# Query projection with its gate columns last: the attention of the last head set moved into the gate units, in a two-block fp32 kernel on one core

## The chip, the cores and the metric

One core of a Trainium2 chip runs one launch. The metric is the device time of that launch in microseconds, the median of several runs. All matrix products are fp32 in three passes (see below), for one sequence of 256 tokens and a model width of 2048, so the kernel streams some 0.5 GB of weights from HBM once and the tensor engine works through them.

## What is computed

Two transformer-like blocks one after the other. The change touches the second half of the first block, a dilated window attention with a gate, and the work for the second block that is carried along beside it:

```python
# first block, attention layer (x is 256 x 2048; 16 heads of 128 in each of 3 dilation groups)
proj = rmsnorm(x, norm_b) @ w_in_b            # 2048 x 8192
q_all, gate = proj[..., :3*2048], proj[..., 3*2048:]
for g, (window, dilation) in enumerate(DILATED_PAIRS):
    q = apply_rope(q_all[:, :, g], cos, sin)
    o_g, lse_g = dilated_window_attention(q, k_shared, v_shared, window, dilation)
alpha = softmax(stack(lses), axis=0)
merged = sum(alpha * stack(outs))
x = x + (merged * silu(gate)) @ w_out_b
# for the second block: three products of silu(c) with ada_w (2048 x 3*2048, 2048 x 2*2048, 2048 x 3*2048)
shift, scale, gate = split(silu(c) @ ada_w + ada_b)
```

## The kernel before

**Units and blocks.** Every weight matrix is cut into blocks of 512 output columns, and a block into four units of 1 MB (four chunks of 128 rows by 512 columns, held as 128x2048). A unit is processed in two halves of two chunks. SyncE loads it into `raw[n % 2]`; ScalarE rounds a half to `w_hi` (`split_hi`, the instruction at L847); VectorE subtracts, `w_lo = raw - w_hi` (`split_lo`, L1426); TensorE then does 24 matmuls of 128x512 for the unit (`product`, L441), three for each chunk and each of the two token tiles. `w_hi` and `w_lo` have two slots as well: a half of unit n+2 can be written only when TensorE has finished that half of unit n (`half_used`). So in the step of unit q all engines work at units q (TensorE) and q+2 (ScalarE, VectorE).

**Banks.** A block sums into one of two pairs of PSUM banks, by the parity of its number. Before its first unit `product` waits (L417) until both tiles of the block two before it have been read out (`bank_free`).

**The query product `in_b`** has 16 blocks, in four sets of four: gate, group 0, group 1, group 2 of one set of four heads. The gate block is taken by ScalarE with a Silu into `gates` (which lies over the residual `res`, spilled to HBM before that and reloaded later), the other three are roped by VectorE (`rope`: four pieces a block, each three reads of PSUM and an add) into `rbuf`, turned by TensorE (`turn_q`) and copied by ScalarE to `q_t`. The four heads of a set are worked on during the 16 units of the next set, by the table `HEAD_STEPS`: in the step of each unit, after its matmuls, TensorE does `scores` (12 small matmuls, L578), `turn` (three transposes of the probabilities, L481) or `weigh` (L488 to L490). VectorE's part of the step comes first in its queue: for `weigh` it multiplies out (`take_out`, L1737), for `scores` it adds the mask (`mask_scores`, L1709); then it splits unit q+2, does one Ada step, and after that the maxima (L1715) or, one step after the scores, the sums over groups (`add_groups`, L1723 on).

**The last set's heads** run by `TAIL_STEPS` within the first six units of the output product `out_b`, whose unit order is changed for it, and from its step 6 on one after the other, with no matmuls of the product between them. `turn_heads` transposes the gated heads of a set, which become the input `xb` of `out_b`.

**Ada units.** 256 units of 512 KB hold the matrices of the second block's modulation. VectorE multiplies each with the silu row and sums (`add_ada`, L1437), one Ada unit beside one weight unit, from the first product to the end of `in_uz`; `ADA0` names the first Ada block of each stage. Four Ada columns are closed by `take_ada`. A load of an Ada unit is issued by SyncE behind the weight unit's and waits until the unit two before it has been used.

**Order.** Nothing is scheduled by a planner: every engine has one in-order queue, written out by hand with semaphores; sets 1 to 3 of `in_b` are one loop body.

Of the kernel before, what the change touches and what calls it, by code (L numbers as in the profile page):

```python
# [11 lines left out]
P = 128  # L12
# [55 lines left out]
def half_of(a, n, i):  # L68
# [13 lines left out]
TAIL_STEPS = {1: [("scores", 0)], 3: [("turn", 0), ("scores", 1)], 4: [("weigh", 0)],  # L82
              5: [("turn", 1), ("scores", 2)],
              6: [("weigh", 1), ("turn", 2), ("scores", 3), ("weigh", 2), ("turn", 3), ("weigh", 3)]}
# [11 lines left out]

HEAD_USES, TAIL_USES = uses_of(HEAD_STEPS), uses_of(TAIL_STEPS)

# [32 lines left out]
ADA0 = {"in_a": 0, "out_a": 4, "kv": 6, "in_b": 10, "out_b": 18, "in_v": 20, "in_uz": 24}  # L131
# [58 lines left out]
def build(nc, x, units, ada_units, vectors, tables, masks, pools, rope_2, spatial, norm_row, c_row, ln_rows, g_kr, g_qr, out):  # L190
    with ExitStack() as ctx:
# [52 lines left out]
        gates = res  # L244
# [30 lines left out]
        weighted, squared = sem("weighted"), sem("squared")  # L275
        factor_ready, scaled = sem("factor_ready"), sem("scaled")
# [32 lines left out]
        def _(sp):  # L309
# [43 lines left out]
            n0, m0 = UNIT0["grp"] + 4, UNIT0["grp"] + 2  # L353
# [4 lines left out]
            n0, pairs = n0 + 4, (ADA_UNITS - m0) // 2  # L358
            with Loop(sp, pairs) as j:
# [3 lines left out]
            n0 += 2 * pairs  # L363

            sp.dma_start(mask[:, 0:640], rope_2).then_inc(mask_in, 16)
            with Loop(sp, (UNITS - n0) // 2) as j:
                for i in range(2):
                    load_unit(n0 + i, 2, j)
            assert (UNITS - n0) % 2 == 0
# [29 lines left out]
        def _(pe):  # L399
# [166 lines left out]
            def turn_q(g, group, j):  # L566


                pe.wait_ge(roped, 5 + g + 3 * j + (3 if group >= 6 else 0))
                for i in range(2):  # L570
                    turn(g0 + group + i, tiles(rbuf, 2 * P * i), 8, j)

            def scores_1(h, k, j):

                for t, groups in ((0, (0, 1, 2)), (1, (0, 1)), (1, (2,))):
                    bank, n = use(k, 20, j), (t + 1) * P
# [6 lines left out]
            def head_part(part, h, uses, j):  # L583

                k = k0 + uses[part, h]
                if part == "scores":
                    if h == 0:
                        for g in (g0 + 4, g0 + 5):

                            pe.wait_ge(turn_free[g % 2], g // 2 + 2 + 4 * j)  # L590
                    scores_1(h, k, j)
                elif part == "turn":
                    turn_probs(use(k, 20, j), 1 + h + 4 * j, ubuf_flat)
                else:

                    weigh(use(k, 20, j), k0 + uses["turn", h], 10 * j, (4 * j + h) * P)

            def turn_heads(group, uses, j):

                k = k0 + uses["weigh", 3]  # L600
                pe.wait_ge(small_free[k % 2], k // 2 + 2 + 10 * j)
                for i in range(2):
                    turn(g0 + group + i, tiles(heads_out, 2 * P * i), 8, j)

            def set_step(q, j, heads):

                if heads:
                    if q == 1:
                        turn_q(2, 4, j)
                    for part, h in HEAD_STEPS.get(q, ()):  # L610
                        head_part(part, h, HEAD_USES, j)
                if q == 11:
                    turn_q(0, 6 if heads else 0, j)
                if q == 15:
                    turn_q(1, 8 if heads else 2, j)
                if q == 15 and heads:
                    turn_heads(10, HEAD_USES, j)
# [4 lines left out]

            for b in range(4):
                product("in_b", b, xa, then=lambda q: set_step(4 * b + q, 0, False), before=None if b else await_rows)
            with Loop(pe, 3) as j:
                for b in range(4):
                    product("in_b", 4 + b, xa, bs=4, us=16, j=j, then=lambda q: set_step(4 * b + q, j, True))

            def tail_step(q):

                if q == 0:
                    turn_q(2, 4, 3)
                for part, h in TAIL_STEPS.get(q, ()):
                    head_part(part, h, TAIL_USES, 3)


            for b in range(2):
                product("out_b", b, xb, qs=range(3), n0=3 * b, then=lambda q: tail_step(3 * b + q))
            tail_step(6)
            turn_heads(6, TAIL_USES, 3)  # L640
            for g in (TURN0["xg"] - 2, TURN0["xg"] - 1):
                pe.wait_ge(turn_free[g % 2], g // 2 + 2)
            for b in range(2):
                product("out_b", b, xb, qs=(3,), n0=6 + b)
# [7 lines left out]
            product("out_b", 2, xb, then=turn_sum)  # L652
            product("out_b", 3, xb, then=lambda q: turn_sum(4 + q) if q < 2 else None)
# [182 lines left out]
        def _(act):  # L836
            steps = Chain(act, act_steps)

            def split_hi(n0, us=0, j=0):
# [3 lines left out]
                act.wait_ge(raw_in[n0 % 2], 16 * (n0 // 2 + 1) + 8 * us * j)  # L843
                for i in range(2):
                    if n0 >= 2:
                        act.wait_ge(half_used, 2 * (n0 - 2) + i + 1 + 2 * us * j)
                    act.activation(half_of(w_hi, n0, i), half_of(raw, n0, i), ACT.Copy).then_inc(hi_done, 1)  # L847
# [198 lines left out]
            def copy_q(g, group, j):  # L1046
                for i in range(2):
                    at = NT * NB + (4 * g + 2 * i) * S
                    copy_turned(g0 + group + i, side_flat[:, at:at + 2 * S], gs=8, j=j)

            def split_heads(group, j):
                for i in range(2):
                    hi_of(g0 + group + i, lambda cc: chunk(xb, 4 * j + 2 * i + cc), gs=8, j=j)

            def set_step(q, j, heads):

                if heads:
                    for part, h in HEAD_STEPS.get(q, ()):
                        if part == "turn":
                            copy_probs(k0 + HEAD_USES[part, h], 20, j)  # L1060
                split_hi(UNIT0["in_b"] + q + 2 + (16 if heads else 0), 16, j)
                if q == 4:

                    b0 = BLOCK0["in_b"] + (4 if heads else 0)
                    act.wait_ge(half_used, 2 * (UNIT0["in_b"] + 4 + (16 if heads else 0)) + 32 * j)
                    for t in range(NT):
                        at = (j + 1 if heads else 0) * NB
                        dst = gates[:, t, at:at + NB] if isinstance(at, int) else gates[:, t, bass.ds(at, NB)]
                        act.activation(dst, banks[2 * (b0 % 2) + t][:], ACT.Silu, scale=stat[:, 4 + t:5 + t])\
                            .then_inc(bank_free[b0 % 2], 1)  # L1070
                if heads:
                    if q == 1:
                        copy_q(2, 4, j)
                    for part, h in HEAD_STEPS.get(q - 1, ()):
                        if part == "scores":
                            exponents(1 + h + 4 * j, ubuf_flat, 768)
                if q == 11:
                    copy_q(0, 6 if heads else 0, j)
                if q == 15:
                    copy_q(1, 8 if heads else 2, j)  # L1080
                if q == 15 and heads:
                    split_heads(10, j)

            act.wait_ge(spilled, 16)
            for q in range(16):
                set_step(q, 0, False)
                if q == 2:

                    act.wait_ge(root_row, 1)
                    act.activation(rows[:], rows[:], ACT.Sqrt, bias=eps).then_inc(root_row, 1)  # L1090
            with Loop(act, 3, steps) as j:
                for q in range(16):
                    set_step(q, j, True)
            for q in range(6):
                if q < 5:
                    split_hi(UNIT0["out_b"] + q + 2)
                if q == 0:
                    copy_q(2, 4, 3)
                for part, h in TAIL_STEPS.get(q, ()):
                    if part == "turn":  # L1100
                        copy_probs(k0 + TAIL_USES[part, h], 20, 3)
# [1183 lines left out]
```

## Time and profile before

| | |
|---|---|
| median of 3 runs | 2192.15 us (2191.84 to 2194.24) |
| the profiled execution | 2189.68 us, its span 2188.0 us, granted TensorE clock 0.986 |
| TensorE busy | 2110.7 us, 96% of the span, 9732 matmuls and transposes |
| VectorE, ScalarE busy | 1574.4 us (72%), 1097.3 us (50%) |
| chain of work that ended last | TensorE 86%, VectorE 5%, ScalarE 4%, issue 2%, DMA 2% |
| HBM read | 518.01 MB, 239 GB/s over the span |

The span is nearly all TensorE. Its idle time is what an edit of the order can win, and it has to be looked up by stretch of time: the page gives 40 slices, and two slices near the middle (the 18th and the 20th) show less than nine tenths of TensorE. The trace shows which instruction stood there and who released it. In the trace a matmul's end is modelled and overlaps the next; the distance from start to start is its cost, about 0.227 us for 128x512 at full clock.

### The profile page before, as it was taken

How to read it: one execution, taken by the hardware profiler on the slowest of the kernel's cores; microseconds unless marked ns; L12 is line 12 of the kernel's file. 1: busy time of each engine (PE TensorE's matmuls, PEld its weight loads, DVE VectorE, ACT ScalarE, POOL GpSimd, SP SyncE). 2: the span in 40 equal slices, each digit the busy share in tenths (PEclk: the TensorE clock that was granted, in tenths of full speed). 3: DMA queues.
4: the chain of work that ended last, by engine and by line, in shares of the span. 5: the costliest groups of instructions: out<-in, count | busy, mean ns of one | idle time of the engine just before them, and what ended most of it. 6: DMA issues, size and time to landing. Idle time of an engine off the chain costs nothing.

```text
span 2188.0 us, 29739 instructions
## 1 busy us (share of the span) xinstructions
PE 2110.7 (96%) x9732; PEld 1746.1 (80%) x9732; DVE 1574.4 (72%) x2506; ACT 1097.3 (50%) x1683; POOL 11.6 (1%) x25
## 2 busy tenths in 40 slices
PE   7999999999999999979899999999999979999988
PEld 6888888888887878757788888888888868878867
DVE  5766777787879888857787778778765565556654
ACT  5444554445444444436544445454444365867742
POOL 0000000000000000000000000000000000000000
PEclk9999999999999999979999999999999989999999
DMA  7876678878766666647688777778744536433333
GB/s 294 293 281 252 239 276 320 301 283 289 264 254 235 228 256 227 222 166 259 232 296 297 289 296 298 278 293 285 301 185 173 192 125 240 173 131 139 136 134 134
DMA packets 93395, 523.34 MB, mean 239 GB/s; under 512 B 10337, under 2 KB 10593, under 8 KB 47489
## 3 DMA queue, kind: packets, MB, share of 16 engines
q1 hardware_dynamic: 90736, 509.60, 63.8%
q0 software_dynamic: 2032, 8.46, 1.1%
q10 hardware_dynamic: 544, 4.19, 0.5%
q8 instruction: 51, 0.84, 0.1%
q14 instruction: 32, 0.25, 0.0%
HBM read 518.01 MB, written 4.19 MB: 239 GB/s over the span
## 4 chain that ended last, share of the span: by engine, by line
PE 86%; DVE 5%; ACT 4%; issue 2%; DMA 2%; DVEq 0%; SPq 0%; ACTq 0%
PE bank L441 78%; PE bank L459 2%; DMA raw<-units 2%; DVE w_lo L1426 1%; PE bank L578 1%; ACT w_hi L847 1%; DVE ada_raw L1437 1%; PE bank L682 1%; PE bank L481 0%; PE bank L784 0%; PE bank L782 0%; PE bank L475 0%; PE bank L515 0%; DVE rbuf L1542 0%; PE bank L488 0%
## 5 line engine op out<-in xcount | busy, mean ns | idle before, releaser
L847 ACT ACTIVATE w_hi<-raw 128x1024 fp32r<-128x1024 f32 (+2 forms) x702 | 726.0, 1047 | 899.2 <-PE bank L441 665.8
L1426 DVE TENSOR_TENSOR w_lo<-raw,w_hi 128x1024 fp32r<-128x1024 f32 (+2 forms) x702 | 832.9, 1207 | 409.5 <-ACT w_hi L847 407.1
L441 PE MATMUL bank<-w_hi,xa_hi 128*128 128x512 f32 x1952 | 770.9, 395 | 5.6 <-DVE w_lo L1426 2.8
L441 PE MATMUL bank<-w_hi,xa_lo 128*128 128x512 f32 x1952 | 761.6, 390 | 0.0
L441 PE MATMUL bank<-w_lo,xa_hi 128*128 128x512 f32 x1952 | 761.2, 390 | 0.0
L441 PEld LDWEIGHTS bank<-w_hi,xa_hi 128*128 128x128 f32 x1952 | 367.7, 188 | 82.8 <-issue 6.1
L441 PEld LDWEIGHTS bank<-w_hi,xa_lo 128*128 128x128 f32 x1952 | 367.2, 188 | 77.6
L441 PEld LDWEIGHTS bank<-w_lo,xa_hi 128*128 128x128 f32 x1952 | 367.7, 188 | 74.6
L441 PE MATMUL bank<-w_hi,xb_hi 128*128 128x512 f32 (+2 forms) x864 | 336.9, 390 | 6.6 <-DVE rbuf L1563 3.6
L441 PE MATMUL bank<-w_hi,xb_lo 128*128 128x512 f32 (+2 forms) x864 | 330.2, 382 | 0.0
L441 PE MATMUL bank<-w_lo,xb_hi 128*128 128x512 f32 (+2 forms) x864 | 330.0, 382 | 0.0
L441 PEld LDWEIGHTS bank<-w_hi,xb_hi 128*128 128x128 f32 x864 | 165.0, 191 | 37.5 <-DVE rbuf L1563 4.0
L441 PEld LDWEIGHTS bank<-w_hi,xb_lo 128*128 128x128 f32 x864 | 164.4, 190 | 29.8
L441 PEld LDWEIGHTS bank<-w_lo,xb_hi 128*128 128x128 f32 x864 | 164.9, 191 | 28.8 <-issue 0.7
L1437 DVE CUSTOM_DVE_ANT_0 ada_raw<-ada_raw,silu_row,ada_acc 128x1024 f32<-128x1024 f32 x128 | 163.6, 1278 | 0.1
L1437 DVE CUSTOM_DVE_ANT_0 ada_raw<-ada_raw,silu_row 128x1024 f32<-128x1024 f32 x128 | 155.9, 1218 | 2.1 <-ACT silu_row L956 2.1
L927 ACT ACTIVATE small<-bank 128x384 f32<-128x384 f32 x32 | 15.7, 491 | 103.8 <-PE bank L481 103.8
L459 PE MATMUL bank<-tab,rbuf 128*128 128x128 f32 (+1 forms) x248 | 34.4, 279 | 9.4 <-DVE rbuf L2045 5.4
L578 PE MATMUL bank<-wide,side 128*128 (+2 forms) x192 | 38.9, 347 | 3.5 <-DVE small L1709 3.0
L459 PEld LDWEIGHTS bank<-tab,rbuf 128*128 128x128 f32 (+1 forms) x248 | 28.8, 139 | 15.7 <-DVE rbuf L2045 5.5
L578 PEld LDWEIGHTS bank<-wide,side 128*128 128x128 f32 x192 | 29.7, 199 | 8.5 <-DVE small L1709 5.0
L2121 DVE TENSOR_TENSOR small<-bank,mask 128x384 f32<-128x384 f32 x16 | 8.9, 557 | 37.0 <-PE bank L784 23.5
(237 smaller groups left out, 1241.3 us busy)
## 6 DMA issues: line engine op xcount, KB each, us to landing
raw<-units SPq DMA_DIRECT2D x351, 1024.0 KB, 4.8
ada_raw<-ada_units SPq DMA_DIRECT2D x256, 512.0 KB, 5.5
rows<-ln_rows POOLq DMA_DIRECT2D x8, 512.0 KB, 3.8
res<-x SPq DMA_DIRECT2D x4, 512.0 KB, 7.6
held<-res ACTq DMA_DIRECT2D x1, 2048.0 KB, 11.9
rows<-norm_row POOLq DMA_DIRECT2D x2, 1024.0 KB, 6.2
res<-held ACTq DMA_DIRECT2D x1, 2048.0 KB, 7.8
out<-res SPq DMA_DIRECT2D x4, 512.0 KB, 7.5
```

The costliest lines, as they stand in the source:

```text
L441: last = pe.matmul(ps[t][:, 0:cols], l, r, start=c == 0 and k == 0, stop=c == CPU * units_of - 1 and k == 2)
L459: last = pe.transpose(bank[0:n, at:at + P], src, ident)
L578: last = pe.matmul(bank[:, i * n:(i + 1) * n], q_t[:, 4 * g + h, t * P:(t + 1) * P], at_(keys_flat, (4 * j + h) * S, n), start=True, stop= ...
L682: last = pe.matmul(bank[:, i * S:(i + 1) * S], ws[:, i * P:(i + 1) * P], vmix[:, t, bass.ds(NB * j + i * S, S)], start=True, stop=True)
L847: act.activation(half_of(w_hi, n0, i), half_of(raw, n0, i), ACT.Copy).then_inc(hi_done, 1)
L927: act.activation(probs_t, small_bank[k0 % 2][:, 0:384], ACT.Copy).then_inc(small_free[k0 % 2], 1)
L1426: dve.tensor_tensor(half_of(w_lo, n0, i), half_of(raw, n0, i), half_of(w_hi, n0, i), ALU.subtract)\
L1437: dve.tensor_tensor_reduce(out=ada_raw[m0 % 2][:], in0=ada_raw[m0 % 2][:], in1=silu_row[:, m0 % 2 * 2 * NB:(m0 % 2 + 1) * 2 * NB], scale=1 ...
L2121: dve.tensor_tensor(small[:, 0:384], small_bank[k % 2][:, 0:384], mask[:, 0:384], ALU.add)\
```

## The change

- `in_b` now computes 12 query blocks first (four sets of three, 12 units each) and the four gate blocks last (16 units). The heads of set j-1 run in the 12 units of set j; those of the last set run in the gate units. `HEAD_STEPS` is a new, tighter table, and `TAIL_STEPS` and the changed unit order of `out_b` are gone.
- `take_out` writes un-gated heads into rows (`weighed`, over `res`) with one scalar factor. After each gate block ScalarE puts Silu into `rbuf` (`take_gate`) and VectorE multiplies (`apply_gate`) into `heads_out`; TensorE turns that (`turn_heads`). For the last gate block all this falls into the first unit of `out_b`. The reload of `res` is issued by ScalarE's queue in the second.
- VectorE's rope of group 0 is spread over the steps of units 4 to 7, one piece each, that of group 1 over units 9 and 10, that of group 2 over the first step of the next set.
- Ada units go by the table `ADA_STEPS`: eight in a set of 12 units, none beside the gate units; the 32 that are left over go to the eight blocks of `out_g`, which had none.
- `in_b` is written out on all engines, with no loop.

```diff
-HEAD_STEPS = {2: [("scores", 0)], 5: [("turn", 0), ("scores", 1)], 6: [("weigh", 0)],
-              8: [("turn", 1), ("scores", 2)], 9: [("weigh", 1)], 11: [("turn", 2), ("scores", 3)],
-              12: [("weigh", 2)], 13: [("turn", 3)], 14: [("weigh", 3)]}
-TAIL_STEPS = ...
+HEAD_STEPS = {2: [("scores", 0)], 4: [("turn", 0), ("scores", 1)], 5: [("weigh", 0)],
+              6: [("turn", 1), ("scores", 2)], 7: [("weigh", 1)], 8: [("turn", 2), ("scores", 3)],
+              9: [("weigh", 2)], 10: [("turn", 3)], 11: [("weigh", 3)]}
+SET_UNITS, GATE_UNITS = 12, 16
-ADA0 = {"in_a": 0, "out_a": 4, "kv": 6, "in_b": 10, "out_b": 18, "in_v": 20, "in_uz": 24}
+ADA0 = {"in_a": 0, "out_a": 4, "kv": 6, "in_b": 10, "out_b": 14, "in_v": 16, "in_uz": 20, "out_g": 28}
+ADA_STEPS = [{0: 1, 1: 1, 2: 1, 3: 1, 5: 1, 7: 1, 8: 1, 11: 1}] + 3 * [{1: 2, 2: 1, 3: 1, 8: 1, 10: 1, 11: 2}] + [{}]
...
# TensorE
+            def set_step(j, q):
+                if j and q == 1:
+                    turn_q(2, j - 1)
+                for part, h in HEAD_STEPS.get(q, ()) if j else ():
+                    head_part(part, h, j - 1)
+                if j < 4 and q in (8, 11):
+                    turn_q((q - 8) // 3, j)
+                if j == 4 and q in (5, 9, 13):
+                    turn_heads((q - 5) // 4)
...
+            for j in range(4):
+                for b in range(3):
+                    product("in_b", 3 * j + b, xa, then=lambda q: set_step(j, 4 * b + q),
+                            before=None if j or b else await_rows)
             for b in range(4):
+                product("in_b", 12 + b, xa, then=lambda q: set_step(4, 4 * b + q))
+            product("out_b", 0, xb, before=await_heads, then=lambda q: turn_heads(3) if q == 0 else None)
...
# ScalarE
+            def take_gate(b):
+                act.wait_ge(half_used, 2 * (UNIT0["in_b"] + 4 * SET_UNITS + 4 * b + 4))
+                if b:
+                    act.wait_ge(gated, b)
+                par = (GATE_BLOCK0 + b) % 2
+                for t in range(NT):
+                    act.activation(rbuf[:, t, :], banks[2 * par + t][:], ACT.Silu, scale=stat[:, 4 + t:5 + t]) ...
...
+                if q == 0:
+                    take_gate(3)
+                elif q == 1:
+                    split_heads(3)
+                    act.wait_ge(gated, 4)
+                    act.dma_start(res[:], held).then_inc(reloaded, 16)
...
# VectorE
+                for part, h in now:
+                    k = k0 + 20 * (j - 1) + HEAD_USES[part, h]
                     if part == "weigh":
+                        take_out(h, k, j - 1)
                     elif part == "scores":
+                        mask_scores(k)
+                if j and q == 0:
+                    rope_query(j - 1, 2, ((0, 0), (0, S)))
+                lo_half(n, 0)
+                for part, h in now:
                     if part == "scores":
+                        maxima(k0 + 20 * (j - 1) + HEAD_USES[part, h])
+                for part, h in before:
+                    if part == "scores":
+                        add_groups(h, j - 1)
+                lo_half(n, 1)
+                if j and q == 0:
+                    rope_query(j - 1, 2, ((1, 0), (1, S)))
+                if j < 4 and 4 <= q < 8:
+                    rope_query(j, 0, ((q // 2 - 2, q % 2 * S),))
+                if j < 4 and q in (9, 10):
+                    rope_query(j, 1, ((q - 9, 0), (q - 9, S)))
+                if j == 4 and q in (4, 8, 12):
+                    apply_gate(q // 4 - 1)
+                if j == 4 and q in (5, 9, 13):
+                    split_heads((q - 5) // 4)
+                for i in range(ADA_STEPS[j].get(q, 0)):
+                    add_ada(m + i)
...
-                after("out_g", n)
+                after("out_g", n, ada=8 * ADA0["out_g"] + 4 * n, then={3: lambda: take_ada(ADA0["out_g"] + n // 2)} if n % 2 else None)
```

## Rows read from the trace of the kernel before

**Rows 1.** Windows: us, busy time of each engine (instructions), granted clock, DMA share, GB/s

```profile
499.65:588.51 88.86, 88.86 (x403) 73.73 (x402) 70.82 (x103) 42.89 (x47) 0.00 (x0) 1.00 0.78 283
588.51:694.62 106.11, 104.36 (x503) 86.42 (x502) 91.00 (x168) 50.98 (x68) 0.00 (x0) 1.00 0.66 242
...
906.73:948.93 42.20, 39.69 (x189) 32.35 (x188) 34.38 (x70) 16.31 (x25) 0.00 (x0) 1.00 0.60 218
948.93:976.65 27.72, 13.44 (x59) 10.53 (x59) 15.61 (x36) 7.94 (x17) 0.00 (x0) 0.66 0.34 126
976.65:1036.62 59.97, 59.97 (x264) 49.11 (x264) 39.39 (x49) 34.37 (x62) 0.00 (x0) 0.96 0.66 242
```

**Rows 2.** Chain in order of time: start, us, engine and line, instructions

```profile
411.03 43.54 PE bank L441 x192
...
712.12 2.02 PE bank L578 x12
...
730.51 0.33 PE bank L481 x3
730.84 2.14 PE bank L578 x12
...
738.47 0.22 PE bank L488 x2
...
811.95 0.87 PE bank L459 x8
```

**Rows 3.** Waits of TensorE, 590 to 977 us: releaser, total us, times, longest

```profile
PE bank L578 <- DVE small L1709: 3.0, 3, 1.0
PE bank L459 <- ACT side L881: 2.3, 3, 0.8
```

**Rows 4.** Timeline of VectorE in set 2: start, us, line, op, idle before

```profile
739.30 0.61 DVE L1737 SCALAR_TENSOR_TENSOR side<-bank,stat,res 128x128 f32<-128x128 f32 x2 [0.69 <-PE bank L490]
739.82 2.35 DVE L1426 TENSOR_TENSOR w_lo<-raw,w_hi 128x1024 fp32r<-128x1024 f32 x2
742.09 1.22 DVE L1437 CUSTOM_DVE_ANT_0 ada_raw<-ada_raw,silu_row 128x1024 f32<-128x1024 f32 x1
...
743.24 0.28 DVE L1723 TENSOR_TENSOR small<-small 128x128 f32<-128x128 f32 x1
...
744.51 1.20 DVE L1426 TENSOR_TENSOR w_lo<-raw,w_hi 128x1024 fp32r<-128x1024 f32 x1
...
758.05 0.42 DVE L1529 TENSOR_TENSOR rbuf<-bank,tab 128x256 f32<-128x256 f32 x1
...
758.59 0.28 DVE L1533 TENSOR_TENSOR ubuf<-bank,tab 128x128 f32<-128x128 f32 x1
...
759.36 0.42 DVE L1529 TENSOR_TENSOR rbuf<-bank,tab 128x256 f32<-128x256 f32 x1
```

**Rows 5.** A split on ScalarE's timeline; a 128x512 product among VectorE's groups

```profile
738.51 1.06 ACT L847 ACTIVATE w_hi<-raw 128x1024 fp32r<-128x1024 f32 x1 [1.66 <-PE bank L441]
...
L1989 DVE TENSOR_TENSOR ubuf<-ubuf,rbuf 128x512 f32<-128x512 f32 x16 | 10.3, 687 | 0.1
```

**Rows 6.** Timeline of TensorE around three idle times

```profile
914.36 1.23 PE L459 MATMUL bank<-tab,rbuf 128*128 128x128 f32 x8 [1.91 <-DVE xb_lo L1486]
...
1927.96 1.97 PE L459 MATMUL bank<-tab,rbuf 128*128 128x128 f32 x8 [4.29 <-DVE rbuf L2045]
...
2133.32 0.79 PE L441 MATMUL bank<-w_hi,xb_hi 128*128 128x512 f32 x1 [3.60 <-DVE rbuf L1563]
...
2138.61 0.53 PE L441 MATMUL bank<-w_hi,xb_hi 128*128 128x512 f32 x1
```

**Rows 7.** Timeline of ScalarE while the residual is spilled to HBM

```profile
345.57 2.01 ACT L847 ACTIVATE w_hi<-raw 128x1024 fp32r<-128x1024 f32 x2 [6.81 <-DMA raw<-units]
```

**Rows 8.** Timelines of VectorE and ScalarE at the end of `out_g`

```profile
1772.16 1.29 DVE L1568 TENSOR_TENSOR res<-res,rbuf 128x512 f32<-128x512 f32 x2
...
1774.96 0.61 ACT L908 ACTIVATE side<-res 128x512 f32<-128x512 f32 x1
```

More of the change, by code:

```diff
@@ L357, in _ @@
             sp.dma_start(mask[:], masks).then_inc(mask_in, 16)
-            n0, pairs = n0 + 4, (ADA_UNITS - m0) // 2
-            with Loop(sp, pairs) as j:
+            with Loop(sp, (UNIT0["in_b"] - UNIT0["out_a"]) // 2) as j:
+                for i in range(2):
+                    load_unit(UNIT0["out_a"] + 4 + i, 2, j)
+                    load_ada(m0 + i, 2, j)
+            n0, m0 = UNIT0["in_b"] + 4, 8 * ADA0["in_b"] + 2
+            for table in ADA_STEPS:
+                for q in range(SET_UNITS if table else GATE_UNITS):
+                    load_unit(n0)
+                    n0 += 1
+                    for _ in range(table.get(q, 0)):
+                        load_ada(m0)
+                        m0 += 1
+            with Loop(sp, (UNIT0["out_g"] - UNIT0["out_b"]) // 2) as j:
                 for i in range(2):
@@ L362, in _ @@
                     load_ada(m0 + i, 2, j)
-            n0 += 2 * pairs
+            n0, m0 = UNIT0["out_g"] + 4, 8 * ADA0["out_g"] + 2
             sp.dma_start(mask[:, 0:640], rope_2).then_inc(mask_in, 16)
+            with Loop(sp, (ADA_UNITS - m0) // 2) as j:
+                for i in range(2):
+                    load_unit(n0 + i, 2, j)
+                    load_ada(m0 + i, 2, j)
+            n0 += ADA_UNITS - m0
             with Loop(sp, (UNITS - n0) // 2) as j:
@@ L591, in head_part @@
                     scores_1(h, k, j)
                 elif part == "turn":
-                    turn_probs(use(k, 20, j), 1 + h + 4 * j, ubuf_flat)
+                    turn_probs(use(k), 1 + h + 4 * j, ubuf_flat)
                 else:
[L596 to L601, printed above, removed]
+                    weigh(use(k), k0 + 20 * j + HEAD_USES["turn", h], 0, (4 * j + h) * P)
@@ L602, in turn_heads @@
+            def turn_heads(b):
+                pe.wait_ge(gated, b + 1)
                 for i in range(2):
[L603 to L617, printed above, removed]
+                    turn(g0 + 24 + 2 * b + i, tiles(heads_out, 2 * P * i))
@@ L623, in _ @@
             for b in range(4):
[L624 to L634, printed above, removed]
@@ L637, in _, with await_heads @@
[L637 to L644, printed above, removed]
+                product("in_b", 12 + b, xa, then=lambda q: set_step(4, 4 * b + q))
+            def await_heads(q):
+                for i in range(2):
+                    g = g0 + 24 + 2 * q + i
+                    pe.wait_ge(turn_free[g % 2], g // 2 + 2)
@@ L650, in turn_sum @@
                 turn(TURN0["xg"] + g, tiles(res, 2 * P * g))
-            product("out_b", 2, xb, then=turn_sum)
-            product("out_b", 3, xb, then=lambda q: turn_sum(4 + q) if q < 2 else None)
+            for b in range(1, 4):
+                product("out_b", b, xb, then=lambda q: turn_sum(2 * b - 2 + q) if q < 2 else None)
             for g in (6, 7):
@@ L1044, in _, with copy_q @@
             k0, g0 = SMALL0["in_b"], TURN0["q"]
-            def copy_q(g, group, j):
+            def copy_q(g, j):
                 for i in range(2):
                     at = NT * NB + (4 * g + 2 * i) * S
-                    copy_turned(g0 + group + i, side_flat[:, at:at + 2 * S], gs=8, j=j)
-            def split_heads(group, j):
-                for i in range(2):
[L1053 to L1099, printed above, removed]
+                    copy_turned(g0 + 6 * j + 2 * g + i, side_flat[:, at:at + 2 * S])
@@ L1740, in take_out, with rope_query @@
                 last.then_inc(small_free[k % 2], 1)
-            def before_split(q, table, uses, j):
-                for part, h in table.get(q, ()):
-                    k = k0 + uses[part, h]
+            def rope_query(j, g, pieces):
+                n = 3 * j + g
+                b0 = BLOCK0["in_b"] + n
+                dve.wait_ge(half_used, 2 * (UNIT0["in_b"] + 4 * n + 4))
+                dve.wait_ge(turned, g0 + 2 * n)
+                rope([banks[2 * (b0 % 2) + t] for t in range(NT)], b0, 0, 0, pieces)
@@ new lines, in apply_gate, with split_heads @@
+            def apply_gate(b):
+                dve.wait_ge(bank_free[(GATE_BLOCK0 + b) % 2], read_out(GATE_BLOCK0 + b))
+                if b == 3:
+                    dve.wait_ge(small_free[(k0 + 79) % 2], small_read(k0 + 79))
+                for t in range(NT):
+                    last = dve.tensor_tensor(heads_out[:, t, :], weighed[:, t, b * NB:(b + 1) * NB], rbuf[:, t, :], ALU.mult)
+                last.then_inc(gated, 1)
+            def split_heads(b):
+                for i in range(2):
+                    lo_of(g0 + 24 + 2 * b + i, xb, 4 * b + 2 * i, HI0["o"] + 2 * b + i + 1)
@@ L1746, in before_split, with set_step @@
+            def set_step(j, q, m):
+                n = UNIT0["in_b"] + SET_UNITS * j + q + 2
+                now, before = (HEAD_STEPS.get(i, ()) if j else () for i in (q, q - 1))
+                for part, h in now:
+                    k = k0 + 20 * (j - 1) + HEAD_USES[part, h]
                     if part == "weigh":
-                        take_out(h, k, j)
+                        take_out(h, k, j - 1)
                     elif part == "scores":
-                        mask_scores(h, k, j)
@@ L1751, in after_split @@
-            def after_split(q, table, uses, j):
-                for part, h in table.get(q, ()):
-                    if part == "scores" and not (table is TAIL_STEPS and q == 5):
-                        maxima(h, k0 + uses[part, h], j)
-                for part, h in table.get(q - 1, ()):
-                    if part == "scores":
-                        add_groups(h, j)
-            def split_heads(group, j):
-                for i in range(2):
-                    lo_of(g0 + group + i, xb, 4 * j + 2 * i, HI0["o"] + i + 1, gs=8, hs=2, j=j)
@@ new lines, in set_step @@
+                if j < 4 and q in (9, 10):
+                    rope_query(j, 1, ((q - 9, 0), (q - 9, S)))
+                if j == 4 and q in (4, 8, 12):
+                    apply_gate(q // 4 - 1)
+                if j == 4 and q in (5, 9, 13):
+                    split_heads((q - 5) // 4)
+                for i in range(ADA_STEPS[j].get(q, 0)):
+                    add_ada(m + i)
+            m0 = 8 * ADA0["in_b"]
+            for j in range(5):
+                for q in range(SET_UNITS if j < 4 else GATE_UNITS):
+                    if j == 1 and q == 0:
+                        dve.wait_ge(spilled, 16)
+                    set_step(j, q, m0)
+                    m0 += ADA_STEPS[j].get(q, 0)
+                    if j == 0 and q == 1:
+                        dve.wait_ge(row_in, 16)
+                        dve.tensor_tensor(rows[:], rows[:], rows[:], ALU.mult).then_inc(root_row, 1)
+                if j < 4:
+                    take_ada(ADA0["in_b"] + j)
@@ L2246 @@
         blocks(a["w_k"], a["w_v"]),
-        blocks(*[w_in_b[:, i * D:(i + 1) * D] for i in (3, 0, 1, 2)]),
-        out_b[out_order],
+        blocks(*[w_in_b[:, i * D:(i + 1) * D] for i in range(3)]),
+        units(w_in_b[:, 3 * D:], NB, CPU),
+        out_b,
         blocks(a_w_in[:, 2 * D:4 * D]),
```

226 lines of the change are left out of this document (98 added, 128 removed).

## The prediction, made before the changed kernel was run

> **What bounds the kernel now.** The page first: TensorE is busy for 96% of the span, so an edit of the order can win or lose only the time in which TensorE stands. I cut the span into stretches, one for each set of `in_b` and for the parts of `out_b` [rows 1]. The first set (16 units, no heads) is all TensorE: 88.86 us. The three sets with heads take 106.1 us each (the second and third repeat the row, up to 906.73). Then come the 42.2 us in which `out_b` runs its first units beside the heads of the last set, 27.7 us with TensorE at work for only 13.4 and a granted clock of 0.66, and 60 us of plain `out_b`. The chain gives the prices of TensorE's work [rows 2]: 192 matmuls in 43.54 us, so 5.44 for a unit of 24; scores 2.02, a turn with scores behind it 0.33 + 2.14 = 2.47, a weigh 3 x 0.22 = 0.67, a turned pair 0.87. The four heads of a set are 2.02 + 3 x 2.47 + 0.33 + 4 x 0.67 = 12.4. A check on the first set: 16 x 5.44 + 2 x 0.87 = 88.8, as the row has it.
>
> **What the change removes.** A set of before holds 87.1 + 12.4 + 4 x 0.87 = 103.0 us of work and takes 106.1; 3.1 are lost. The waits name 3.0 + 2.3 = 5.3 us for the three sets together [rows 3]: the third bank of the fourth head's scores waits for VectorE, and the gated heads' turn waits for a bank that ScalarE is copying. Both go, since the scores are spread otherwise and the heads' turn no longer follows another turn: 5.3. The other 1.3 or so of a set (slower steps at the change of instruction kinds) goes with the heads and stays. From 906.73 to 1036.62 it is 129.9 us for 16 units, the heads, a pair of q, the pair of gated heads and six half pairs of sums: 87.1 + 12.4 + 0.9 + 0.9 + 2.6 = 103.9. Of the 26.0 lost, 1.3 stay; 24.7 go. All TensorE work is the same in number after the change. **Removed: 30.0 us.**
>
> **The new wait at unit 8 of each set.** A set now has three blocks. Block 2 (units 8 to 11) needs the banks of block 0 (units 0 to 3), and these are read out by four pieces of rope in VectorE's steps 4 to 7. The last piece stands in step 7 behind the second half of the split of unit 9, and this half can't be rounded before TensorE has finished unit 7. So TensorE reaches unit 8 before the piece has begun, whatever VectorE's load. In set 0, from the end of unit 7: ScalarE begins 0.04 later (738.47 to 738.51) and takes 1.06 [rows 2, 5], the subtraction 1.20, the three reads of a rope piece 758.05 to 758.87 = 0.82 [rows 4], a semaphore about 0.1: 3.2 us. In sets 1 to 3 step 7 begins with `take_out(1)`, which waits for the weigh behind unit 7. In the trace the same step stands at 738.47: the weigh follows the unit, `take_out` starts at 739.30, the next split at 739.82, 1.35 after the unit's end [rows 4]. Then half of unit 9, 1.14 (2.27 for the two), `add_groups(2)`, 1.27 (743.24 to 744.51), the second half, 1.14, and the reads, 0.82: 5.7 after the unit's end, with the semaphore 5.8, against the 0.5 at which the next matmul would be issued behind the weigh. 5.3 us, three times. The sum is 3.2 + 15.9 = **19.1 us**, all on TensorE's path. Queued behind that wait are all later matmuls, and so everything.
>
> **The boundary between sets.** VectorE had 91.0 us of work in 106.1 [rows 1]; it now has, for 12 units, 12 x 2.27 + 8 x 1.15 for Ada + 12 pieces of rope at 1.3 + some 20 for heads = 72 in a set with 80 of TensorE's work, but unevenly. From the end of unit 9 in a set with heads (us after it): split begins 1.35, half 2.5, sums 3.8, half 4.9, two pieces of rope 7.5. Step 10: the split of unit 12 waits until ScalarE, which first copies the probabilities of the turn behind unit 10, has rounded it, 8.0; both halves 10.3, two pieces 12.9, Ada 14.1. TensorE ends unit 11 at 0.67 + 5.44 + 0.33 + 5.44 = 11.9, its weigh at 12.5, and waits 0.4 for rope. Step 11 and step 0 of the next set in VectorE's queue: `take_out` 14.6, two halves 16.9, two Ada units 19.2, `take_ada` 19.6, two pieces 22.2, two halves 24.5, two pieces 27.1. TensorE turns at 13.8, does two units until 24.7 and wants the third turned pair: 2.4 us wait. Sets 1 to 3 pay the 0.4 at their end, sets 2, 3 and the gate units the 2.4, and set 1, behind a set with no heads and one Ada unit in step 11, about 0.8: 1.2 + 7.2 + 0.8 = **9.2 us**. The least is near nothing, if the queues overlap a little better (the nearest row is `out_b`'s first unit, where the same turn waits 1.91 for VectorE after four pieces of rope [rows 6]); the most is 14, if the second Ada unit of step 11, whose load is issued only when step 10's is used, comes late by 1.6.
>
> **The first unit of `out_b`.** `turn_heads(3)` stands behind unit 0, and needs `apply_gate(3)`, which stands in VectorE's step 0 behind the second half of a split that again waits for the end of the unit. ScalarE 1.1, half 1.2, Ada 1.15, two products 128x512 at 0.69 [rows 4, 5]: **4.9 us**. ScalarE's Silu lies beside the unit's matmuls and costs nothing; if that cover were gone it would be some 1.3. The same steps in the gate units have a whole unit between product and turn and are hidden, at 0.
>
> **The clock.** After 1.91 us idle a turn of eight takes 1.23, little over the usual [rows 2, 6]. After 4.29 us it takes 1.97: that stretch is at the lower level, 1.2 GHz instead of 2.4. After 3.60 us thirteen matmuls, until 2138.61, run at the lower level, at 0.43 instead of 0.23: 2.6 lost. The three waits of 5.3 and the one of 4.9 are longer than either. I take 2.0 each, between the about 1.4 and the 2.6: **8.0 us**, bounds 3 and 12.
>
> **What is moved elsewhere.** Ada: 32 steps leave `in_b`'s shorter sets and its gate units and land in `out_g`, where VectorE works 57% of the time; 1.15 more in each 5.44 is hidden by the matmuls, and the load beside a weight unit is what `in_b` had in its first set, 283 GB/s with no wait [rows 1]. Only the last Ada step and `take_ada` of `out_g` come before the last residual add, some 1.5 us; that add ended at 1773.4 while ScalarE, busy with its own part, took up its result at 1774.96 [rows 8]: +0.2, bounds 0 and 1.6. SyncE's queue: an Ada load waits for its buffer in front of the next unit's load, but in sets 1 to 3 only where VectorE is late itself. The 2 MB reload of the residual used to run while TensorE stood; now it meets two streams. Its nearest row is the spill, during which ScalarE waited 6.81 us for a weight unit [rows 7], with almost all of it taken up by the unit ahead: +1.0, bounds 0 and 4. The Trainium skill (Trainium Kernel Development and Optimization, Key Constraints) says that the DMAs of all queues run on the same 16 engines and interleave, which speaks against issuing this reload beside the loads; the row agrees. Without that rule this term would be 0. Writing `in_b` out instead of looping and Exp no longer alternating with Silu on ScalarE's tables are free: neither stands on the path.
>
> **Sum:** -30.0 + 19.1 + 9.2 + 4.9 + 8.0 + 0.2 + 1.0 = +12.4 us. The profiled execution took 2189.68, so 2202.1; the median of the three runs is 2.5 higher, 2192.15, and the forecast is 2192.15 + 12.4 = 2204.6 us.
>
> **Rivals.** (1) *The clock holds through waits of 5 us.* Then 8.0 go: 2196.6, at the edge of slower. Against it stand both rows of 3.60 and 4.29. 12%. (2) *The boundary is worse*: the second Ada unit is late, the waits before the third turned pair pass 4 us and cost clock too, and the reload costs its most: +5 + 4 + 3: 2216. For it: two Ada units in one step, with one of the loads issued 4 us before. 15%. (3) *VectorE's queue is shorter than I add up*, so that at unit 8 only the forced 3.2 us remain in every set and the boundary is 1: -30.0 + 12.8 + 1 + 4.9, 2.0 of clock for `out_b` alone, and 1.2, make -8.1: 2184, faster. It decides once `take_out` to the last read takes under some 3 us in all; against it, my durations are already from start to start. 8%. (4) *It doesn't do what it says*: the last set's attention is not covered by the gate units, since its probabilities wait for a Silu and a table change on ScalarE; then part of the 24.7 comes back, over 2210; 3%. (5) A mild mix, clock at its least and boundary near nothing, is 2192, no change: 8%. The forecast itself has 54%.
>
> **The numbers.** The range must reach from the mild mix to rival 2: 2190 to 2218. A difference under 0.2% (4.4 us) can't be told from none here. Faster: rival 3 and a little of the mix, 0.09. Within 0.2%: the rest of the mix and half of rival 1, 0.14. Slower: 0.77.
>
> **What would show it.** Right: in each set one idle time of TensorE before a matmul, released by VectorE's L1529 to L1533 kind (rope), 3.2 us in set 0 and 5.3 in the next three, with some ten matmuls at 0.63 long behind each; a turn behind unit 1 waiting 2 us for rope; 4.9 us before the turn in `out_b`; nothing of the old 27.7 us stretch. Wrong: no idle time at unit 8; matmuls at 0.39 long right behind it; or `out_g` longer than before.

## The result

The changed kernel takes 2205.14 us, median of 5 runs (2204.34 to 2207.32), against 2192.15 (2191.42 to 2197.85): a ratio of 1.006, 95% interval 1.0048 to 1.0072. It is 13.0 us slower. The forecast was 2204.6.

The profile after, first the stretches: most of set 0 (its first 65.6 us), two of the sets with heads, the gate units with the last set's heads, and `out_b` to its end. Columns: us; busy time of TensorE, weight loads, VectorE, ScalarE and GpSimd with their instructions; granted clock, DMA share, GB/s.

```profile
500.42:566.00 65.58, 62.45 (x281) 51.48 (x280) 47.13 (x68) 30.17 (x34) 0.00 (x0) 1.00 0.73 258
...
657.50:749.50 92.00, 84.04 (x398) 69.70 (x397) 70.82 (x141) 35.24 (x50) 0.00 (x0) 0.96 0.51 183
749.50:841.50 92.00, 84.42 (x398) 69.94 (x397) 70.93 (x142) 36.23 (x51) 0.00 (x0) 0.96 0.51 183
841.50:950.00 108.50, 105.98 (x517) 88.58 (x517) 76.17 (x133) 56.57 (x79) 0.00 (x0) 1.00 0.49 175
950.00:1057.48 107.48, 95.66 (x428) 78.24 (x426) 72.98 (x96) 56.77 (x96) 0.53 (x1) 0.95 0.73 267
```

The 27.7 us in which TensorE worked for 13.4 [rows 1] are gone: the gate units hold the last set's heads and TensorE is busy for 98% of them. But each set of 12 units, 80 us of work, takes 92, with a clock of 0.96 where before it was 1.00. Who is waited for, on TensorE from 499 to 1060 us (releaser: us in total, times, longest):

```profile
PE bank L462 <- DVE ubuf L1534: 18.3, 4, 5.1
PE bank L480 <- DVE rbuf L1543: 7.9, 6, 2.6
PE bank L480 <- DVE side L1755: 4.8, 1, 4.8
```

None of the three is in [rows 3]. The first line is a matmul (L462 is `product`) that waits for the last PSUM read of a rope piece, once in each of the four sets; the second, turned pairs that wait for rope; the third, the turn in `out_b` that waits for `apply_gate`. How the first looks, in set 0 and in set 2, on TensorE's timeline (start, us, line; idle before):

```profile
547.34 0.50 PE L462 MATMUL bank<-w_hi,xa_hi 128*128 128x512 f32 x1 [3.13 <-DVE ubuf L1534]
547.67 0.39 PE L462 MATMUL bank<-w_lo,xa_hi 128*128 128x512 f32 x1
...
721.11 0.80 PE L462 MATMUL bank<-w_hi,xa_hi 128*128 128x512 f32 x1 [5.06 <-DVE ubuf L1534]
721.70 0.63 PE L462 MATMUL bank<-w_lo,xa_hi 128*128 128x512 f32 x1
...
726.40 0.56 PE L462 MATMUL bank<-w_hi,xa_hi 128*128 128x512 f32 x1
726.80 0.39 PE L462 MATMUL bank<-w_lo,xa_hi 128*128 128x512 f32 x1
```

Behind 3.13 us of idling the matmuls go on at full speed; behind 5.06 they run at 1.2 GHz, at 0.43 us from start to start instead of 0.23, for twelve instructions and a part of the thirteenth. VectorE's step 7 in set 1 shows why TensorE stands. This is its timeline, in the order of the code: `take_out` behind the weigh, half of unit 9, the sums of `add_groups`, the other half, and only then the piece of rope whose third operation frees the bank at 629.12. Unit 8 starts at 629.18.

```profile
624.26 0.61 DVE L1737 TENSOR_SCALAR res<-bank,stat 128x128 f32<-128x128 f32 x2 [0.67 <-PE bank L511]
624.78 1.22 DVE L1420 TENSOR_TENSOR w_lo<-raw,w_hi 128x1024 fp32r<-128x1024 f32 x1
625.92 0.28 DVE L1724 TENSOR_TENSOR small<-small 128x128 f32<-128x128 f32 x1
...
627.19 1.20 DVE L1420 TENSOR_TENSOR w_lo<-raw,w_hi 128x1024 fp32r<-128x1024 f32 x1
628.31 0.42 DVE L1530 TENSOR_TENSOR rbuf<-bank,tab 128x256 f32<-128x256 f32 x1
...
628.84 0.28 DVE L1534 TENSOR_TENSOR ubuf<-bank,tab 128x128 f32<-128x128 f32 x1
```

In `out_b`, on VectorE and then on TensorE: the product that is waited for stands behind the second half of unit 2's split (956.73, itself waiting for the end of unit 0) and an Ada step.

```profile
956.73 1.22 DVE L1420 TENSOR_TENSOR w_lo<-raw,w_hi 128x1024 fp32r<-128x1024 f32 x1 [1.43 <-ACT w_hi L854]
957.87 1.22 DVE L1439 CUSTOM_DVE_ANT_0 ada_raw<-ada_raw,silu_row 128x1024 f32<-128x1024 f32 x1
...
959.01 1.29 DVE L1755 TENSOR_TENSOR side<-res,rbuf 128x512 f32<-128x512 f32 x2
```

```profile
960.36 1.97 PE L480 MATMUL bank<-tab,side 128*128 128x128 f32 x8 [4.76 <-DVE side L1755]
961.98 0.78 PE L462 MATMUL bank<-w_hi,xb_hi 128*128 128x512 f32 x1
```

### The profile page after: what moved, and what is told of

The parts are those of the page before. It is cut to its first block, busy times and chain, and to the rows that moved or that the text cites. A ratio compares the mean times of both kernels' runs of the same rounds, so it can differ in the third digit from the quotient of the medians.

```text
span 2203.5 us, 28792 instructions
## 1 busy us (share of the span) xinstructions
PE 2115.0 (96%) x9732; PEld 1750.3 (79%) x9732; DVE 1579.4 (72%) x2514; ACT 1091.2 (50%) x1679; POOL 11.6 (1%) x25
## 4 chain that ended last, share of the span: by engine, by line
PE 85%; DVE 6%; ACT 4%; DMA 3%; issue 2%; SPq 0%; ACTq 0%; DVEq 0%
PE bank L462 77%; DMA raw<-units 3%; PE bank L480 2%; DVE w_lo L1420 2%; PE bank L599 2%; ACT w_hi L854 1%; PE bank L691 1%; DVE ada_raw L1439 1%; PE bank L502 0%; PE bank L793 0%; DVE rbuf L1530 0%; PE bank L791 0%; PE bank L496 0%; DVE rbuf L1543 0%; PE bank L536 0%
## 5 line engine op out<-in xcount | busy, mean ns | idle before, releaser
L462 PE MATMUL bank<-w_hi,xa_hi 128*128 128x512 f32 x1952 | 776.6, 398 | 24.6 <-DVE ubuf L1534 18.3
L462 PE MATMUL bank<-w_hi,xa_lo 128*128 128x512 f32 x1952 | 765.4, 392 | 0.0
L462 PE MATMUL bank<-w_lo,xa_hi 128*128 128x512 f32 x1952 | 765.0, 392 | 0.0
L462 PEld LDWEIGHTS bank<-w_hi,xa_hi 128*128 128x128 f32 x1952 | 370.2, 190 | 103.1 <-DVE ubuf L1534 19.3
L462 PEld LDWEIGHTS bank<-w_hi,xa_lo 128*128 128x128 f32 x1952 | 369.4, 189 | 78.7
L462 PEld LDWEIGHTS bank<-w_lo,xa_hi 128*128 128x128 f32 x1952 | 370.3, 190 | 75.1
L462 PE MATMUL bank<-w_hi,xb_hi 128*128 128x512 f32 (+2 forms) x864 | 336.4, 389 | 7.0 <-DVE rbuf L1564 3.6
L462 PE MATMUL bank<-w_lo,xb_hi 128*128 128x512 f32 (+2 forms) x864 | 329.9, 382 | 0.0
L462 PE MATMUL bank<-w_hi,xb_lo 128*128 128x512 f32 (+2 forms) x864 | 329.9, 382 | 0.0
L462 PEld LDWEIGHTS bank<-w_hi,xb_hi 128*128 128x128 f32 x864 | 164.6, 190 | 38.4 <-DVE w_lo L1420 5.2
L462 PEld LDWEIGHTS bank<-w_hi,xb_lo 128*128 128x128 f32 x864 | 164.2, 190 | 29.8
L462 PEld LDWEIGHTS bank<-w_lo,xb_hi 128*128 128x128 f32 x864 | 164.4, 190 | 29.2 <-issue 1.0
L1710 DVE TENSOR_TENSOR small<-bank,mask 128x384 f32<-128x384 f32 x16 | 8.9, 557 | 55.3 <-PE bank L599 55.3
L599 PE MATMUL bank<-wide,side 128*128 128x128 f32 (+1 forms) x192 | 36.4, 335 | 0.0
L2116 DVE TENSOR_TENSOR small<-bank,mask 128x384 f32<-128x384 f32 x16 | 8.9, 557 | 38.0 <-PE bank L793 24.5
## 6 DMA issues: line engine op xcount, KB each, us to landing
held<-res ACTq DMA_DIRECT2D x1, 2048.0 KB, 13.4
```

Of the source, the lines that this page charges most:

```text
L462: last = pe.matmul(ps[t][:, 0:cols], l, r, start=c == 0 and k == 0, stop=c == CPU * units_of - 1 and k == 2)
L1710: dve.tensor_tensor(dst, src, m, ALU.add).then_inc(small_free[(k + i) % 2], 1)
L2116: dve.tensor_tensor(small[:, 0:384], small_bank[k % 2][:, 0:384], mask[:, 0:384], ALU.add)\
```

## The experiments

All times stand against the 2205.14 us of the changed kernel, and each ratio is to the kernel before, measured beside it. The changed kernel was not measured again beside the experiments; the kernel before was, with medians of 2192.68 and 2193.54 instead of 2192.15, so that a gain is uncertain by about 1 us from this alone.

**Are the banks given back too late, or has VectorE too much to do?** The same rope pieces, one step earlier:

```diff
-                if j < 4 and 4 <= q < 8:
-                    rope_query(j, 0, ((q // 2 - 2, q % 2 * S),))
+                if j < 4 and 4 <= q < 7:
+                    rope_query(j, 0, (((0, 0),), ((0, S),), ((1, 0), (1, S)))[q - 4])
```

> The four rope pieces of group 0 stand in VectorE's steps 4, 5, 6 and 6 instead of 4 to 7; the number of instructions on every engine is the same. Theory (the banks of block 0 are given back too late for unit 8): the four idle times before unit 8 (3.3, 5.2, 5.2, 5.2 us in the changed kernel) go, and with them the twelve to fourteen matmuls at the lower clock behind three of them (2.4 to 2.8 us each); step 6 ends some 0.6 us later than the next weigh, which a whole unit covers. Time 2205.1 - 18.9 - 7.6 = 2179 us. Rival (VectorE has too much to do in 12 units, whatever its order): the same work is left, the wait only moves to another place in the set, and the time stays within 3 us of 2205.

2180.03 us (2177.74 to 2181.22), ratio 0.9945 (0.9929 to 0.9962). The waits before unit 8 fall from 18.3 us to 1.1: none in set 0, and 0.4 us (0.5 from start to start) in each of the three sets with heads. The other two lines are as they were:

```profile
PE bank L480 <- DVE rbuf L1543: 7.6, 6, 2.2
PE bank L480 <- DVE side L1755: 4.8, 1, 4.8
...
PE bank L462 <- DVE ubuf L1534: 1.1, 3, 0.4
```

What is left stands before unit 8 itself, behind the weigh of unit 7, and still waits for the last read of the rope; the matmuls behind it are at full speed:

```profile
619.72 0.50 PE L462 MATMUL bank<-w_hi,xa_hi 128*128 128x512 f32 x1 [0.40 <-DVE ubuf L1534]
```

25.1 us for moving one piece of 1.3 us by one step: it was the order, not the load. VectorE has exactly as much to do. The sum agrees: 19.0 less the 1.6 that is left, and 7.6 of clock, make 25.0.

**The wait in `out_b`.**

```diff
+                if q == 0:
+                    apply_gate(3)
                 if q != 15:
                     split_lo(n0 + 2 + q)
                     add_ada(m0 + q)
-                if q == 0:
-                    apply_gate(3)
```

> In the first step of out_b VectorE applies the last gate block before it splits unit 2, instead of after the split and the Ada step. Theory (the turn behind unit 0 waits for a product that stands behind a split that itself waits for unit 0): the product is done about 4 us into the unit, the 4.9 us of idle time and the eight or so slow matmuls and the slow turn behind it go: 4.9 + 2.5 = 7.4, time 2197.7 us. Rival (ScalarE's Silu and its part of the step are what is late): the wait stays and the time stays at 2205.

2197.23 us (2194.39 to 2200.22), ratio 1.0024 (1.0015 to 1.0034). 7.9 less, the wait is gone; ScalarE's Silu was in time. One thing came with it, and it is taken up below under the reload: ScalarE now waits 4.5 us for a weight unit just behind the reload of `res`.

**The slow matmuls behind the waits.**

```diff
+                if 0 < j < 4 and q == 7:
+                    await_turn_bank(g0 + 6 * j)
+                    for _ in range(22):
+                        pe.matmul(turn_bank[(g0 + 6 * j) % 2][:], xa[0][:, 0, 0:P], ...)
```

> In the three sets with heads TensorE does 22 matmuls of 128x512 into a bank that is free (their result is overwritten) behind the weigh of unit 7, some 5.0 us of work within the 5.2 us wait for the banks; everything else is as changed. Theory (the slow matmuls behind the wait are the lower clock that follows TensorE's idling): unit 8 starts when it did, but at full speed: 2.4 + 2.4 + 2.8 = 7.6 us less, time 2197.5 us. Rival (they are slow for another reason, such as the banks or the reads that VectorE does just then, or the clock has nothing to do with this idling): no change, 2205 us.

2197.53 us (2194.71 to 2203.38), ratio 1.0028 (1.0017 to 1.004). 7.6 less, by giving TensorE more to do; the intervals of the two kernels leave some 3 us either way. In the profiles the stretch is 6.4 us shorter, with 1.5 us of clock lost in set 0 that the changed kernel's profile did not lose. Its timeline in set 1: the added matmuls (L634) fill the wait, and those of unit 8 are at full speed from the first.

```profile
623.37 5.28 PE L634 MATMUL bank<-xa_hi 128*128 128x512 f32 x22
628.67 0.50 PE L462 MATMUL bank<-w_hi,xa_hi 128*128 128x512 f32 x1
629.01 0.40 PE L462 MATMUL bank<-w_lo,xa_hi 128*128 128x512 f32 x1
```

**The boundary between sets.** A first try took the Ada steps off the sets with heads and put two beside a unit elsewhere:

```diff
-ADA_STEPS = [{0: 1, 1: 1, 2: 1, 3: 1, 5: 1, 7: 1, 8: 1, 11: 1}] + 3 * [{1: 2, 2: 1, 3: 1, 8: 1, 10: 1, 11: 2}] + [{}]
+ADA_STEPS = [{0: 2, 1: 2, 2: 2, 3: 2, 4: 1, 5: 1, 6: 1, 7: 1, 8: 2, 11: 2}] + 3 * [{}] + [
+    {1: 1, 2: 1, 3: 1, 8: 1, 10: 2, 11: 2, 12: 2, 13: 2, 14: 2, 15: 2}]
...
```

Left out are the loop of the loads and the place of `take_ada`, which follow the table.

> The 32 Ada steps of in_b stand in set 0 (16) and beside the gate units (16), none in the three sets with heads; the same number in all. Theory (the wait before the third turned pair, 2.7, 2.3 and 2.3 us, is VectorE's backlog at the end of a set, of which 3 Ada steps and one late Ada load are 4 us; the 0.5 us before the second pair is not): the 7.4 us go, the 0.5 us three times and all waits before unit 8 stay. Time 2205.1 - 7.4 = 2197.7 us. Rival (VectorE's load as a whole sets the pace of these sets): the waits before unit 8 shrink too, by up to the 8 x 1.15 = 9.2 us of each set, and the time falls below 2190.

2209.17 us (2206.85 to 2210.03), ratio 1.0077 (1.006 to 1.0094): a miss. The three waits before the third turned pair did go (one of 0.8 came in set 1, which had none), and the waits of 5.2 us before unit 8 stayed to the hundredth, so the rival falls too. But the new places cost more than that. In the first 100 us of `in_b` VectorE now waits for loads of Ada units, where it waited for none in the changed kernel, and its longest wait for ScalarE is 5.1 us instead of 2.6 (in total it is less, 12.6 instead of 19.4). ScalarE itself waits 20.4 us for weight units there, where it was 7.1:

```profile
DVE w_lo L1421 <- ACT w_hi L855: 12.6, 10, 5.1
...
DVE ada_raw L1440 <- DMA ada_raw<-ada_units: 4.6, 3, 2.8
```

In set 0 the wait before unit 8 grew from 3.3 to 6.5 us and brought the lower clock; at the end of the gate units VectorE was late by so much that the turn in `out_b` waited 11.2 instead of 4.8:

```profile
966.43 1.97 PE L481 MATMUL bank<-tab,side 128*128 128x128 f32 x8 [11.21 <-DVE side L1756]
```

So the steps were spread again, at most one beside a unit:

```diff
+ADA_STEPS = [{q: 1 for q in (0, 1, 2, 3, 4, 5, 6, 7, 8, 11)}] + 3 * [{2: 1, 3: 1, 8: 1}] + [
+    {q: 1 for q in (0, 1, 2, 3, 6, 7, 8, 10, 11, 12, 13, 14, 15)}]
...
```

> Only the Ada steps are moved, at most one beside a unit: 10 in set 0, 3 in each set with heads (units 2, 3, 8), 13 beside the gate units. The first try at this put two beside one unit in set 0 and in the last gate units, and there ScalarE's and VectorE's steps waited for loads. Theory (the wait before the third turned pair is VectorE's backlog, and the backlog is the Ada steps at the end of a set): 7.4 us go and nothing comes elsewhere, time 2197.7 us, idle before unit 8 still 3.3 and three times 5.2. Rival (any Ada step in set 0 beyond eight delays the rope there): the wait before unit 8 of set 0 grows past 3.3 and half of the gain is lost, 2201 or more.

2193.89 us (2193.15 to 2198.79), ratio 1.0006 (0.9997 to 1.0015): 11.2 less. The waits for rope on TensorE fall from 7.9 us to 1.1, those before unit 8 stay at 18.3:

```profile
PE bank L463 <- DVE ubuf L1535: 18.3, 4, 5.1
PE bank L481 <- DVE side L1756: 4.8, 1, 4.8
...
PE bank L481 <- DVE rbuf L1544: 1.1, 3, 0.4
```

The waits explain 7.4 of the 11.2. In the two profiled executions 34 matmuls of the stretch ran at the lower clock against 46, at 0.2 us each 2.4 more. These come behind the same waits, so they look like a spread of the clock and no merit of the edit, but that is argued from one profile of each. The stretch from `in_b` to `in_v` is 9.4 us shorter in the profile; the remainder lies in the rest of the kernel, which varies from profile to profile (see below).

**Do the gains add?** The first two edits, then all three:

> The first two edits together, Ada steps as in the change. If they are independent: 2205.1 - 25.1 - 7.9 = 2172.1 us, with the waits of 2.3 us before three turned pairs still there, and the difference to the kernel with all three edits is the price of these waits, some 7.5 us. If removing one wait presses the next: 2176 or more.

2173.22 us (2171.61 to 2176.09), ratio 0.9911 (0.9898 to 0.9925).

> Three edits of the changed kernel together: the rope of group 0 by step 6, the last gate block applied before the split, and the 32 Ada steps spread by at most one beside a unit (10 in set 0, 3 in each set with heads, 13 beside the gate units). Theory (the waits are separate and each has its own place): the gains add, 25 + 8 as measured for the first two alone and some 7.5 for the third, so 2205.1 - 40.5 = 2164.6 us, 1.3% under the kernel before; what is left are the 0.5 us before a turned pair and before some scores. Rival (the gains overlap, because VectorE has 72 us of work in 80 and each wait removed presses the next): less than 33 us gained, 2172 or more.

2165.09 us (2162.03 to 2166.16), ratio 0.9872 (0.9856 to 0.9887). For the first two, 25.1 + 7.9 = 33.0 stand against 31.9 together. With the third the medians of the single edits make 44.2 against 40.1: the third gave 11.2 alone and 8.1 as the last step. The profiles settle it: in the stretch of `in_b` and `out_b` the three alone save 24.2, 7.4 and 9.4 us, 41.0 in sum, and together 40.0. So the gains add, to about 1 us, and the other 3 us are spread outside this stretch. What is left of the waits at the turned pairs and at unit 8 is 0.5 us three times each; none stands before scores. This version is 1.3% faster than the kernel before. Its whole stretch from the first matmul of `in_b` to that of `in_v`, above the same in the changed kernel and in the kernel before (three answers, us first):

```profile
500.03:1017.06 517.03, 507.63 (x2422) 422.22 (x2420) 407.12 (x718) 252.26 (x361) 0.53 (x1) 1.00 0.61 221
```

```profile
500.42:1057.48 557.06, 518.98 (x2422) 429.82 (x2420) 408.18 (x718) 252.94 (x361) 0.53 (x1) 0.97 0.57 205
```

```profile
499.65:1046.01 546.36, 517.19 (x2421) 426.42 (x2420) 440.81 (x778) 259.38 (x365) 0.53 (x1) 0.97 0.65 240
```

## Why the prediction was right, step by step

The stretch took 557.06 - 546.36 = 10.7 us more in the two profiled executions; the sum for it was 12.2 (12.4 without the 0.2 for `out_g`).

- **Removed, -30.0:** it was about 32.5. The version with all three edits has 3.2 us of small waits left (six of 0.53, from start to start) and takes 29.3 less than before: 32.5. The changed kernel agrees: its new waits of 32.8 and clock loss of 10.2 make 43.0, and 43.0 - 10.7 = 32.3. The step that was off is the 1.3 us of a set of heads that I let stay: about half of it went. With all three edits a set takes 81.97 us from its unit 8 to the next set's (702.62 to 784.59); its work is 80.3 and its two small waits 1.1, which leaves 0.6. What these slower steps were, no experiment shows; that VectorE was just behind TensorE there, rather than a cost of changing the kind of instruction, is only argued.
- **Unit 8, +19.1:** 3.3 + 3 x 5.23 = 19.0 from start to start. The order of the queue and its durations, read in the trace of before for the same instructions in another step, gave it to 0.1 in each set. It is shown by moving the rope to step 6.
- **Boundary, +9.2:** 3 x 0.52 + 2.7 + 2.3 + 2.3 = 8.9; the 0.8 of set 1 did not come. Of the late second Ada unit there is 0.5 us, once. That these waits are VectorE's backlog of Ada steps is shown by spreading them evenly; the first try shows it too, with a bill elsewhere.
- **`out_b`, +4.9:** 4.9, shown by putting the product ahead of the split.
- **Clock, +8.0:** 10.2. Behind the three waits of 5.2 ran 12 to 14 matmuls at the lower level (7.6 us), behind the one of 4.9 a turn of 1.97 and eight matmuls (2.6). I had taken 2.0 each, it was 2.5, near the upper of the two rows [rows 6]. The matmuls added into the waits show that the idling is the cause for the three in the sets, 7.6 us with a forecast of 7.6.
- **Reload, +1.0:** 0. It landed in 9.0 us instead of 7.8, and no engine waited for a weight unit through it. But that was helped by the wait of 4.9 us in front of it: TensorE had stood, and the DMAs moved 290 GB/s during the reload. In the three kernels without that wait the reload took 9.8 to 11.9 us and ScalarE waited 4.5 to 5.7 us for the weight unit behind it, much as beside the spill [rows 7], so that row was a near case after all:

```profile
964.37 2.01 ACT L854 ACTIVATE w_hi<-raw 128x1024 fp32r<-128x1024 f32 x2 [4.52 <-DMA raw<-units]
```

This is from the version with the gate ahead of the split; there the DMAs moved 351 GB/s during the reload. TensorE waited for no weight unit in any of them, so the term of the sum stays 0. The Trainium skill (Trainium Kernel Development and Optimization, Key Constraints) says that DMAs issued from different queues run on the same engines and interleave. The traces agree in that both got slower (a weight unit lands in a median of 6.7 us in the 40 us around that reload, 4.8 in the changed kernel); the rule gives no cost for TensorE, and here there was none.
- **Ada in `out_g`, +0.2:** 0. From `out_g`'s fifth block to the first matmul behind `out_g` it is 1682.10 to 1782.74 before and 1693.41 to 1794.06 after, 100.6 both times. In the last four blocks VectorE has 66.1 us of work now and TensorE no wait:

```profile
1693.41:1780.00 86.59, 86.59 (x385) 71.71 (x384) 66.06 (x85) 32.20 (x35) 0.00 (x0) 1.00 0.78 282
```

- **The rest of the kernel:** not in the sum, and the spans differ by 15.5 us, not by 10.7. The part behind the fifth block of `out_g`, whose code is the same but for the Ada steps, took 505.9 us in the profiled execution of before and 510.1 in that of after; in the seven experiments it was 506.7 to 509.9. From start to start the 4.2 us lie in three places. The first stage behind `out_g` is 1.3 us longer (79.5 against 78.1; 78.4 to 80.2 in the experiments), with TensorE waiting 4.4 us instead of 1.5 for VectorE's split. The clock costs 0.9 more behind a wait of 4.3 us that both have. And behind an idle time of 2.3 us near the end the lower level came in after's execution and not in before's: 2.9 more, of which the next wait gives 0.9 back. The executions profiled also sit differently in their runs, that of before 2.5 us under its median, that of after on it. The agreement of 2204.6 and 2205.1 is thus closer than the terms deserve: 2.3 too little removed, 2.2 too little clock, 1.6 too much elsewhere, and some 2 us of the rest. That they cancel is luck; the terms for unit 8 and `out_b`, right to 0.1, are not.
- **Rivals:** the clock didn't hold (1); the boundary was no worse (2); VectorE's queue was as long as added up (3); the last set's attention is covered by the gate units (4), as their row shows, 106.0 busy of 108.5. The mild mix (5) with its clock at 3 and its boundary at 0 would be 2190.4 and not 2192; nothing else hangs on that.

What is open is why the first stage behind `out_g` got longer in all eight kernels of the new order, and how much of the last 510 us is spread of the clock; no experiment was made on either. That the Ada loads in `out_g` reach into that stage is a possibility that no run tests.

## What to carry to other kernels

When work is packed into fewer units, look first at what gives a PSUM bank back: with two pairs of banks a block has to be read out within the next block, and a read that stands behind a split which waits for that block's last unit is late by construction, however little the engine has to do. Put reads that free a bank ahead of work that waits for the consumer itself; here one rope piece a step earlier and one product ahead of a split together turned 0.6% slower into 0.9% faster. And price a wait of TensorE with what follows it: four waits of 5 us cost 20 us and 10 more at the lower clock.

## What the runs showed of the hardware

- Behind every one of the twelve waits of 5.2 us that were left in four kernels the lower level of the clock held for seven to fourteen matmuls of 128x512, at 0.43 instead of 0.23 us from start to start.
- Behind the waits before the third turned pair (2.17 to 2.63 us by the bracket of the timeline) it came in 3 of 15 cases, in otherwise the same place of the same code. One of them, in the version with the rope by step 6 (the turn of eight takes 1.97 us instead of the usual 1.09):

```profile
745.81 1.97 PE L480 MATMUL bank<-tab,rbuf 128*128 128x128 f32 x8 [2.18 <-DVE rbuf L1543]
```

- The level may fall after the work has begun again: in set 0 of the version with the Ada steps spread evenly, the first five matmuls behind a wait of 3.13 us are fast, and from the sixth on eight are slow. This happened in two of the four kernels with that wait.

```profile
548.14 0.50 PE L463 MATMUL bank<-w_hi,xa_hi 128*128 128x512 f32 x1 [3.13 <-DVE ubuf L1535]
...
548.95 0.39 PE L463 MATMUL bank<-w_hi,xa_hi 128*128 128x512 f32 x1
549.18 0.45 PE L463 MATMUL bank<-w_lo,xa_hi 128*128 128x512 f32 x1
549.42 0.63 PE L463 MATMUL bank<-w_hi,xa_lo 128*128 128x512 f32 x1
```
